# Moving a 31-tap convolution to VectorE alone, its layer norm into attention, and its projections to the front

## The reference

```python
n = rms_norm_2(h, mix_norm[l])
p = n @ w_in[l]
u_conv, q, k, v, q_mem = jnp.split(p, splits, axis=-1)
y_conv = conv_module(u_conv, ...)      # a * sigmoid(gate), 31-tap depthwise causal convolution
                                       # over 384 channels, layer norm over channels, silu
q = apply_rope(rms_norm_2(q...), cos, sin)      # 6 heads of 64
k = apply_rope(rms_norm_2(k...), cos, sin)      # 2 heads of 64
y_swa = sliding_window_attention(q, k, v, sinks)       # window 128
mk, mv = jnp.split(rms_norm_2(mem) @ w_mem_kv[l], 2, axis=-1)
y_mem = memory_attention(rms_norm_2(q_mem), rms_norm_2(mk), mv)      # 4 heads, 256 memory rows
h = h + jnp.concatenate([y_conv, y_swa, y_mem], axis=-1) @ w_out[l]
```

## Time and profile before

| | us |
|---|---|
| runs before: median of 3 | 5424.01 |
| lowest, highest | 5421.43, 5435.53 |
| profiled execution, its own time | 5434.72 |
| profiled execution, span of its trace | 5432.9 |
| mean granted TensorE clock | 0.939 |
| busy: TensorE, VectorE, ScalarE, GpSimd | 5007.7, 1701.7, 1048.4, 153.0 |
| layer 0: first scores of attention to the end of its last output copy | 3527.94 to 3647.95 |
| layer 0: first matmul of the projection behind it | 3669.72 |

### The profile page before, as it was taken

The page is one execution under the profiler, slowest core; times in us unless marked ns, Lnnn a source line. Parts: engine busy times, 40 slices in busy tenths (PEclk is TensorE's granted clock), DMA queues, the critical chain, the costliest instruction groups (busy, mean ns, idle before and its releaser), DMA issues.

```text
span 5432.9 us, 60219 instructions
## 1 busy us (share of the span) xinstructions
PE 5007.7 (92%) x26216; PEld 2632.1 (48%) x26216; DVE 1701.7 (31%) x3322; ACT 1048.4 (19%) x2280; POOL 153.0 (3%) x139
## 2 busy tenths in 40 slices
PE   7978999997989999988999999959999999959998
PEld 4554555553446667643443444424444444424443
DVE  3253111116146666532112112562113111562112
ACT  1042000001035555512001000151001000151000
POOL 0000000000000000000000000050000000050000
PEclk8999999998978998889999999959999999959999
DMA  5300222210100000021221221201221222201220
GB/s 211 147 17 31 78 109 78 109 62 33 41 1 3 2 3 3 2 102 62 78 78 65 77 78 70 85 9 62 78 74 74 77 78 71 92 16 62 78 74 27
DMA packets 26855, 338.45 MB, mean 62 GB/s; under 512 B 3008, under 2 KB 3008, under 8 KB 6752
## 3 DMA queue, kind: packets, MB, share of 16 engines
q1 hardware_dynamic: 23904, 324.51, 15.9%
q0 software_dynamic: 2688, 10.09, 0.5%
HBM read 330.40 MB, written 4.19 MB: 62 GB/s over the span
## 4 chain that ended last, share of the span: by engine, by line
PE 66%; issue 25%; DVE 4%; ACT 3%; POOL 1%; DMA 0%; SPq 0%; POOLq 0%; DVEq 0%; ACTq 0%
PE ps L872 50%; PE ps L1203 2%; PE ps L899 1%; PE ps L1175 1%; PE ps L1134 1%; PE ps L1186 1%; PE ps L1265 1%; POOL arena L801 1%; PE ps L918 1%; PE ps L1124 1%; DVE rstd L1767 1%; PE ps L1252 1%; PE ps L1249 1%; PE ps L988 1%; PE ps L1004 1%
## 5 line engine op out<-in xcount | busy, mean ns | idle before, releaser
L872 PE MATMUL ps<-arena 128*128 128x512 f32 (+3 forms) x9728 | 3826.2, 556 | 93.1 <-DVE arena L2049 30.0
L872 PEld LDWEIGHTS ps<-arena 128*128 128x128 f32 x9728 | 1848.0, 191 | 2062.2 <-issue 1629.6
L1556 ACT ACTIVATE square<-arena 128x512 f32<-128x512 f32 x88 | 55.4, 630 | 1250.7 <-DVE arena L2021 1250.7
L1928 DVE TENSOR_TENSOR arena<-ps,arena 128x512 f32<-128x512 f32 (+1 forms) x136 | 87.7, 645 | 644.7 <-PE ps L872 644.7
L2021 DVE TENSOR_TENSOR arena<-ps,rstd 128x512 f32<-128x512 f32 x88 | 60.8, 691 | 501.4 <-PE ps L872 501.3
L1940 DVE TENSOR_TENSOR arena<-arena,ps 128x384 f32<-128x384 f32 (+1 forms) x96 | 57.5, 599 | 498.9 <-ACT arena L1478 498.9
L1478 ACT ACTIVATE arena<-ps 128x384 f32<-128x384 f32 (+1 forms) x96 | 50.5, 526 | 797.4 <-PE ps L872 797.4
L801 POOL TENSOR_TENSOR arena<-arena 128x512 f32<-128x512 f32 x120 | 143.9, 1228 | 1787.1 <-ACT arena L1400 1787.1
L2026 DVE TENSOR_TENSOR arena<-ps,arena 128x512 f32<-128x512 f32 x88 | 60.9, 692 | 403.3 <-PE ps L872 403.2
L1348 ACT ACTIVATE square<-arena 128x512 f32<-128x512 f32 (+2 forms) x86 | 61.0, 713 | 525.5 <-PE ps L899 224.2
L899 PE MATMUL ps<-square,ones 128*128 128x512 f32 x220 | 99.7, 598 | 51.6 <-ACT square L1348 45.8
(11 more groups left out here) (256 smaller groups left out, 3631.0 us busy)
## 6 DMA issues: line engine op xcount, KB each, us to landing
arena<-in_panels SPq DMA_DIRECT2D x145, 2048.0 KB, 7.7
arena<-in_panels SPq DMA_DIRECT2D x9, 1536.0 KB, 6.4
arena<-in_bias POOLq DMA_DIRECT2D x8, 512.0 KB, 6.4
arena<-in_x_in SPq DMA_DIRECT2D x1, 3072.0 KB, 11.2
x_save<-arena POOLq DMA_DIRECT2D x1, 2048.0 KB, 7.5
arena<-x_save POOLq DMA_DIRECT2D x1, 2048.0 KB, 28.7
out_x<-arena SPq DMA_DIRECT2D x8, 256.0 KB, 2.2
arena<-in_mem_in POOLq DMA_DIRECT2D x1, 1024.0 KB, 30.6
```

Of the source, the lines that this page charges most:

```text
L872: ins = pe.matmul(dest, left(k), right(k), start=(k == 0), stop=(k == nk - 1))
L1928: dve.tensor_tensor(Y[:, c, a:b], bank, Y[:, c, a:b], ALU.add).then_inc(sem("tile_free"), one("tile_free"))
```

## The change

What it does, part by part:

- The order of the column panels of the input projection is changed on the host: convolution chunks first, then q, k, memory q, then v. On all engines `mix_in` becomes 16 steps: 6 convolution tiles, 6 head tiles, 4 tiles of v.
- All 93 taps of a layer (31 x 3) are fused multiply-adds on VectorE. 54 are issued in `mix_in`, 4 to 7 per step from step 2 on (`DVE_TAPS`), and 39 in attention, three per turn in turns 0 to 12. The taps of two channel chunks alternate in most of the order. ScalarE's products and GpSimd's adds are gone, and `tap_product` with them.
- The statistics of the head norm are taken in another way: TensorE multiplies each 128 x 128 block of squares, as weights, with two columns of the block-of-ones matrix, so that the sums of 128 tokens lie on partitions, two columns a block. Scale, square root and reciprocal then work on 128 x 8 instead of 128 x 512. ScalarE spreads the result to 128 x 512, TensorE turns it back by four transposes, and VectorE's product reads it from PSUM. The work of an item is staggered over four steps.
- The sums of the layer norm move into attention: the first sum at turn 14, centring (VectorE) and squares (ScalarE) at turn 15, the second sum at turn 17, the scale at turn 18. What stays in `conv` is square root, reciprocal, gain, sigmoid (with the bias folded in) and one fused product.
- VectorE's output copy of pair i-3 moves ahead of the scores of pair i.
- The first panel of the output projection starts with row chunks 3 to 7 of all four tiles and waits for the convolution only then.

The diff, cut to its core:

```diff
-        add(np.concatenate([q[:, 0], q[:, 1], q[:, 2], w[:, 1152:1280]], 1))
-        add(np.concatenate([w[:, 1408:1664], conv[:, 0], gate[:, 0]], 1))
-        add(np.concatenate([conv[:, 1], gate[:, 1], conv[:, 2], gate[:, 2]], 1))
+        add(np.concatenate([conv[:, 0], gate[:, 0], conv[:, 1], gate[:, 1]], 1))
+        add(np.concatenate([conv[:, 2], gate[:, 2], q[:, 0], q[:, 1]], 1))
+        add(np.concatenate([q[:, 2], w[:, 1152:1280], w[:, 1408:1664]], 1))
...
+        HEAD_ITEMS = {6: [0], 7: [1, 2], 8: [3], 9: [4], 10: [5], 11: [6], 12: [7]}
...
+        DVE_TAPS = {2: 4, 3: 6, 4: 6, 5: 7, 6: 7, 7: 4, 8: 4, 9: 4, 10: 4, 11: 4, 12: 4}
+        PAIR_TAPS = 3
+        LN_MEAN, LN_CENTRE, LN_SQUARES, LN_VAR = 14, 15, 17, 18
+        def tap_order():
+            order = [(0, tap) for tap in range(10)]
+            for tap in range(10, TAPS):
+                order += [(0, tap), (1, tap - 10)]
+            for tap in range(TAPS):
+                order += [(2, tap)] + ([(1, tap + 21)] if tap + 21 < TAPS else [])
+            return order
...
@@ gpsimd
-                        pool.tensor_tensor(conv_y[:, c, :], conv_y[:, c, :], tap_product[c], ALU.add).then_inc(
-                            sem("pool_tap"), one("pool_tap"))
...
@@ tensor, attention
+                    if l is not None and i == LN_MEAN:
+                        pe.wait_ge(sem("tapped"), l + 1)
+                        row_sum(lambda c: conv_y[:, c, :])
+                    if l is not None and i == LN_SQUARES:
+                        pe.wait_ge(sem("ln_square"), 3 * (l + 1))
+                        row_sum(lambda c: Y[:, c, 0:LAT])
...
@@ tensor, project
+                    for m in range(4):
+                        banks.append(tile())
+                        for k in range(3, KD):
+                            pe.matmul(banks[m], w[:, k, m * P:(m + 1) * P], src[:, k, 0:LAT], start=(k == 3), stop=False)
+                    for m in range(4):
+                        for c in range(3):
+                            if m == 0:
+                                pe.wait_ge(sem("convolved"), more("convolved"))
+                            ins = pe.matmul(banks[m], w[:, c, m * P:(m + 1) * P], src[:, c, 0:LAT], start=False, stop=(c == 2))
+                        ins.then_inc(sem("tile_done"), one("tile_done"))
...
@@ tensor, mix_in
+                    for it in HEAD_ITEMS.get(s, ()):
...
+                        for t in range(item_width(it) // P):
+                            ins = pe.matmul(ps[:, stat_bank(it), 2 * t:2 * t + 2], square[:, it % 2, t * P:(t + 1) * P],
+                                            head_ones[:, 0:P:C], start=True, stop=True)
...
+                    for it in HEAD_ITEMS.get(s - 1, ()):
...
+                        for t in range(item_width(it) // P):
+                            ins = pe.transpose(ps[:, 5, t * P:(t + 1) * P], item_spread(it)[:, t * P:(t + 1) * P], ident)
...
@@ scalar, mix_in
+                        act.wait_ge(sem("head_var"), base + it + 1)
+                        act.activation(r, r, ACT.Sqrt).then_inc(sem("head_std"), one("head_std"))
+                        act.wait_ge(sem("head_inverse"), base + it + 1)
...
+                        act.copy(item_spread(it).rearrange("p (a b) -> p a b", b=C),
+                                 r.unsqueeze(2).broadcast_to([P, w // C, C])).then_inc(sem("head_spread"), one("head_spread"))
...
@@ vector
+            def conv_tap(l, c, tap):
...
+                    dve.wait_ge(sem("tap"), len(TAP_ORDER) * l + TAP_ORDER.index((c, tap - 1)) + 1)
+                    ins = dve.scalar_tensor_tensor(conv_y[:, c, :], src, w, conv_y[:, c, :], ALU.mult, ALU.add)
...
@@ vector, attention
+                        if i < LN_MEAN - 1:
+                            next_taps(l, PAIR_TAPS)
+                        elif i == LN_MEAN - 1:
...
+                            last_taps(l)
+                        elif i == LN_CENTRE:
+                            centre(l)
+                        elif i == LN_VAR:
+                            ln_variance(l)
```

More of the change, by code:

```diff
@@ L1009, in attention, with row_sum @@
                 n["unit"] += len(pairs)
+            def row_sum(row):
+                for c in range(3):
+                    ins = pe.matmul(ps[:, 5, :], ones[:, :], row(c), start=(c == 0), stop=(c == 2))
+                ins.then_inc(sem("ln_sum"), one("ln_sum"))
             def project(count, segs, src, dest, ready):
@@ L1297, in mix_in @@
                                lambda k: w[:, k, CTX:2 * CTX])
[L1298 to L1306, removed]
-                    else:
[L1308 to L1318, removed]
@@ L1417, in attention @@
                 for i in range(len(pairs) + 1):
-                    if l is not None and i >= 1:
-                        for tap in range(TAPS * (i - 1) // TAP_STEPS, min(TAPS, TAPS * i // TAP_STEPS)):
-                            conv_tap(l, tap)
+                    if l is not None and i == LN_CENTRE:
+                        for c in range(3):
+                            act.wait_ge(sem("centred"), 3 * l + c + 1)
+                            act.activation(Y[:, c, 0:LAT], conv_y[:, c, :], ACT.Square).then_inc(
+                                sem("ln_square"), one("ln_square"))
                     if i >= 1:
@@ L1693, in conv @@
+                n["tile"] += 4 + CONV_TILES + HEAD_TILES + LAT // P
             def conv(l):
-                act.wait_ge(sem("tapped"), more("tapped"))
-                n["plain_sums"] += 3
-                n["var"] += 1
-                squares(lambda c: conv_y[:, c, :], 3, 0, LAT, lambda c: act.wait_ge(sem("centred"), more("centred")))
+                act.wait_ge(sem("ln_var"), l + 1)
+                act.activation(rstd[:, 0:LAT], rstd[:, 0:LAT], ACT.Sqrt).then_inc(sem("ln_std"), one("ln_std"))
@@ L1884, in attention @@
                             normalise(i - 1, h)
+                    if i >= 3:
+                        dve.wait_ge(sem("output"), base + i - 2)
+                        dve.tensor_copy(pairs[i - 3]["dest"], ps[:, 7, 0:P]).then_inc(sem("attended"), one("attended"))
                     if i < len(pairs):
@@ L1887, in attention @@
                     if l is not None:
[L1888 to L1892 removed]
+                        if i < LN_MEAN - 1:
+                            next_taps(l, PAIR_TAPS)
+                        elif i == LN_MEAN - 1:
+                            assert n["tap"] == len(TAP_ORDER) * (l + 1)
+                            last_taps(l)
[3 more added lines that the diff above has]
+                            ln_variance(l)
                 n["unit"] += len(pairs)
@@ L2328, in mix_in @@
+                dve.wait_ge(sem("normed"), n["normed"])
                 dve.tensor_copy(stat[:, 15:16], q2[:, 0, 0:1]).then_inc(sem("roped"), one("roped"))
             def conv(l):
-                dve.wait_ge(sem("tap"), n["tap"])
-                dve.wait_ge(sem("pool_tap"), more("pool_tap", (TAPS - 1) * len(POOL_CHANNELS)))
-                dve.tensor_copy(stat[:, 15:16], conv_y[:, 0, 0:1]).then_inc(sem("tapped"), one("tapped"))
-                dve.wait_ge(sem("summed"), more("summed", 3))
+                dve.wait_ge(sem("ln_std"), l + 1)
@@ L2336, in conv @@
+                settle(dve.reciprocal(rstd[:, 0:LAT], rstd[:, 0:LAT]))
                 for c in range(3):
[L2337 to L2343 removed]
```

233 lines of the change are left out of this document (134 added, 99 removed).

## The result

The kernel after takes 5282.02 us (median of 4 runs, 5273.76 to 5282.93). The kernel before, timed beside it, takes 5422.82 (4 runs, 5421.43 to 5435.53). The profiled execution took 5282.16 us with a span of 5280.2. Against the span of 5432.9 before, the two traces differ by 152.7 us; the profiled execution of before lay 12 us above its median, and that is the rest.

A forecast was written before the change was run, and what follows sets the result against it. Second-block attention was taken as bound by a chain of handovers, with no engine full. Layer norm 21.5, attention 25 and projections 4 gave 50.5 us a layer, 101 in all: 5323 us against a median of 5424.01, range 5292 to 5370.

The forecast's parts named there:

- works on just these and on the projections before them: Scope: only some 140 us per second-block layer that TensorE does not bound, and the projections before, would change.
- Attention of the second block: Each layer's attention falls from 120.0 to 95 us, a gain of 25.
- The tapped part: Second-block attention, first 13 pairs: three taps each, VectorE-bound at 4.7 us a pair, 60 us in all.
- the untapped pairs: Second-block attention, seven pairs without taps: between 2.5 and 3.5 us each, taken at 3.0, so 21 us.
- the sums: Two layer norm sums moved into attention: 2.6 to 5.1 us each, taken at 4 each, 8 us.
- rival (b): Second-block attention: clock rises at the first sum and holds for untapped pairs; 89 us a layer, total 5310; chance 0.15.
- The layer norm: Gap between attention and projection: 21.8 us serial, hidden under early projection chunks (17.2 us of cover); gain 21.5 a layer.
- the cold start at low clock is there before and after: Start of the output projection behind attention: low clock in both kernels, so no gain was counted.
- Projections: Projections before second-block attention: 2.3 us gained to the last column tile, 1.9 after; together 4, bounds -6 to +8.
- The taps: VectorE's taps in second-block projections and attention: 0.77 us each with GpSimd's adds gone, against a mean of 1.129.
- Rival (f): VectorE's 93 taps a layer cost 2.0 us each instead of 0.77; kernel slower, 5521; chance 0.03.
- (c): Second-block attention pairs bound by the four-engine round trip, not taps; 17 us a layer lost, 5357; chance 0.14.

The follow-up runs named there:

- the cover is taken away: Changed kernel, but the output projection waits for all of the convolution before its first matmul, instead of starting with early row chunks; 5303.51 us, ratio 0.9757.
- the two-tap kernel: Changed kernel with 14 more taps in the projections and the remaining 25 two per pair over thirteen attention pairs; 5267.38 us, ratio 0.9696.
- Two turns of similar length: From the two-tap kernel with ScalarE's three layer norm squares moved behind its exponentials and turned copies; 5262.49 us, ratio 0.9692.

## Why the prediction was wrong where it was, and right where it was

**The step that failed** stands in the first lines: the change "works on just these and on the projections before them", the two layers of the second block, with the first block "untouched" in the description of the reference. But the line "VectorE's output copy of pair i-3 moves ahead of the scores of pair i" is in `attention`, which both blocks call, and only the taps behind it are bound to a layer. The first block's 24 pairs went from 127.1 to 100.8 us: 26.3 us without a term in the sum. With the old order in that block alone the kernel takes 5300.84 us, which lies in the range. The trace of the kernel before could have told: in the stretch of the first block's attention (258.9 to 386) the same wait stood as in the earlier trace rows, this time with no taps to blame:

```profile
PE ps L1004 <- DVE arena L1892: 27.4, 21, 2.2
```

27.4 us of wait, 26.3 us gained. In the first block the copy stood behind VectorE's work on the scores (mask and maximum), which wait for TensorE's scores of the next pair (31.7 us in 21 waits before, 6.5 in 8 after), so TensorE's output matmul stood behind a copy that stood behind TensorE itself.

**Attention of the second block**: forecast 95 us, measured 86.1. The tapped part was right: 13 distances of 4.48 us, 58.2 (3496.19 to 3554.43), against 60. The rest was mis-sized: 27.8 us against 35. I took the untapped pairs at 3.0 and the sums at 4 each; with the clock at 0.91 the pairs took 2.4 (3559.94 to 3562.34) and the sums 3.2 each. By distances from 3554.43 on: 5.5 with the first sum, 2.4, 5.8 with the centring, 5.5 with the second sum, 2.4, and 6.2 to the end. This was rival (b), with 89 us for this stage and a chance of 0.15. I gave it little because the earlier trace rows show 0.52 throughout, but those pairs are all tapped, and the untapped ones had no row. Before, the first block's 0.94 was the nearest row to an untapped pair, and I used it for the rival only. The Trainium skill (TensorE: Matmul & The Clock Gate, "What's actually happening") says that activity releases a throttle which is there by default. The trace agrees: scores take 1.23 us at 3554.43 and 0.70 at 3559.94, behind denser work, and 1.23 again at 3568.15, behind the 2.74 us without work.

**The layer norm**: 21.5 us forecast, 21.7 and 21.3 measured (21.8 to 0.06 in layer 0), with about 9 beneath the early chunks against 8.4 of idle when the cover is taken away. One clause was wrong: "the cold start at low clock is there before and after". The projection's first half-passes took 0.85 us before and take 0.43 now, since the clock is already up when it starts. The stages behind attention gained 2.8 and 3.3 us beyond the norm; the first seven half-passes make 2.8 and 2.7 of it, and the last 0.6 in layer 1 is not explained.

**Projections**: 4 us forecast, 4.8 and 4.4 measured. The parts hold in layer 0: up to the last column tile 8.4 us beyond the tiles, as forecast, and from there to the first scores 13.4, where 14 were forecast. The sums with two columns take 0.12 us per instruction (a run of eight, 0.95 us), as taken from the earlier trace rows, and inside the stretch TensorE waits once for VectorE (0.66 us, at 3457.40) and once for ScalarE (0.65, at 3491.43).

**The taps**: 0.77 us forecast, 700 to 754 ns in all 180 recorded (the first tap of each channel chunk, six in all, is another instruction, a product with a bias and not a fused multiply-add). Rival (f), a tap of 2.0 us, fell, and so did (c): pairs are bound by taps, as the two-tap kernel shows. GpSimd's share can be put down too: 1129 ns with its adds, 749 without. The kernel before shows it by itself: 8 of its 60 recorded taps have no add beside them, and they take 749 to 753 ns. The Trainium skill (GPSIMD Engine Reference, "1. Specifications") says that GpSimd's interfaces to SBUF are shared with VectorE, with contention where a VectorE instruction has two SBUF inputs. The tap has two, and the trace agrees by the numbers just given.

The sum with its errors mended, against the traces' 152.7: 101 forecast, 26.3 for the first block, 9.0 + 8.4 for attention, 6.1 behind it (mostly the cold start), 1.3 for the projections, and 0.6 from the two stretches that the change does not touch: 152.7. Of the range, the lower end of 5292 is 3 us below its own terms (5323 - 28 = 5295); nothing hangs on it.

## What to carry to other kernels

Before a part is called untouched, look at who calls the code that the diff edits; here the move of three lines in a shared loop gave over four tenths of what the whole change gave. When an engine executes in order, a copy that frees another engine's next step belongs ahead of that engine's long or waiting work: read the wait for the copy in every stage that holds it. And a stage that changes from sparse to dense must be costed at both clock levels, since the level moves with the work.

## What the runs showed that I had not expected

The order of one 0.29 us copy gave 67 us in the kernel before by stages (26.3 + 20.7 + 20.5) and 60 by the medians (5426.83 to 5367.18), over four tenths of the whole gain. Two turns of similar length, 4.30 and 3.59 us between scores, left TensorE at the low level in one layer and at the high one in the other; what decides stays open. And a stretch of 3000 us that no kernel here edits lasted from 3025.5 to 3035.6 us in different executions of different kernels; the cause is not known, and effects of under 10 us were read from stages, not from totals.
